# Feed-forward of a decoder trunk: one plain unit, four seven-product units in a row, the half unit last

## The reference

```
def swiglu(x, w_gu, w_down):          # x: 256 x 1024 after an RMS norm
    gate, up = jnp.split(x @ w_gu, 2, axis=-1)      # w_gu: 1024 x 5632
    return (jax.nn.silu(gate) * up) @ w_down        # w_down: 2816 x 1024
```

## Time and profile before

| | |
|---|---|
| device time, median of 3 runs | 2020.74 us (2019.19 to 2021.62) |
| the profiled execution's own time | 2019.88 us |
| its span in the profile | 2018.0 us |
| granted TensorE clock over the span | 1.0 of full (2.4 GHz) |
| PE busy | 1998.2 us, 10299 matmuls |
| DVE, ACT, POOL busy | 1566.5, 1187.3, 168.7 us |

### The profile page before, as it was taken

One profiled execution on the slowest core, in us unless ns is written; L12 is line 12 of the kernel. 1 busy time (PEld: TensorE's weight loads), 2 busy tenths in 40 slices (PEclk: granted clock), 3 DMA queues, 4 the chain that ended last, 5 costly groups with the idle time before them and its releaser, 6 DMA issues.

```text
span 2018.0 us, 25283 instructions
## 1 busy us (share of the span) xinstructions
PE 1998.2 (99%) x10299; PEld 1705.1 (84%) x10299; DVE 1566.5 (78%) x1489; ACT 1187.3 (59%) x1269; POOL 168.7 (8%) x165
## 2 busy tenths in 40 slices
PE   7999999999999999999999999999999999999998
PEld 6888998888888899988888888988888888998887
DVE  6778567778886889968878878778878778568777
ACT  6546576556655676646556555446556556576555
POOL 2000001000000014410001000000001001001000
PEclk9999999999999999999999999999999999999999
DMA  8867535867787484368876867658876867535864
GB/s 275 257 226 229 184 105 138 252 235 229 232 248 210 139 274 132 126 229 239 242 217 194 245 241 193 206 189 248 248 219 188 253 222 232 178 105 142 256 229 114
DMA packets 242183, 419.87 MB, mean 208 GB/s; under 512 B 10668, under 2 KB 92932, under 8 KB 241556
## 3 DMA queue, kind: packets, MB, share of 16 engines
q1 hardware_dynamic: 215732, 363.34, 53.0%
q0 software_dynamic: 26048, 54.61, 15.0%
q10 hardware_dynamic: 288, 0.31, 0.0%
HBM read 417.14 MB, written 1.08 MB: 207 GB/s over the span
## 4 chain that ended last, share of the span: by engine, by line
PE 87%; DVE 7%; ACT 3%; issue 1%; DMA 1%; ACTq 0%; SPq 0%; POOLq 0%; POOL 0%; DVEq 0%
PE bank L1594 51%; PE bank L1735 23%; PE bank L1600 7%; DVE w_lo L1113 3%; PE bank L1769 2%; DVE arena L1461 2%; ACT w_hi L734 2%; PE bank L1627 1%; PE bank L1909 1%; PE bank L1940 1%; DMA stage<-in_ssd_w_in 0%; PE bank L1922 0%; ACT arena L1009 0%; DMA arena<-seg_rows 0%; DMA arena<-in_ffn_norm 0%
## 5 line engine op out<-in xcount | busy, mean ns | idle before, releaser
L1113 DVE TENSOR_TENSOR w_lo<-stage,w_hi 128x2048 fp32r<-128x2048 f32 (+1 forms) x224 | 514.8, 2300 | 152.4 <-ACT w_hi L734 151.2
L1113 DVE TENSOR_TENSOR w_lo<-arena,w_hi 128x2048 fp32r<-128x2048 f32 (+1 forms) x196 | 444.3, 2268 | 162.4 <-ACT w_hi L734 161.7
L734 ACT ACTIVATE w_hi<-stage 128x2048 fp32r<-128x2048 f32 (+1 forms) x224 | 423.3, 1892 | 207.5 <-PE bank L1594 141.7
L734 ACT ACTIVATE w_hi<-arena 128x2048 fp32r<-128x2048 f32 (+1 forms) x196 | 371.7, 1897 | 236.8 <-PE bank L1594 157.0
L1594 PE MATMUL bank<-w_hi,mt_hi 128*128 128x512 f32 x928 | 367.3, 396 | 0.4 <-DVE mt_lo L1347 0.4
L1594 PE MATMUL bank<-w_lo,mt_hi 128*128 128x512 f32 x928 | 361.5, 390 | 0.0
L1594 PE MATMUL bank<-w_hi,mt_lo 128*128 128x512 f32 x928 | 361.0, 390 | 0.0
L1594 PE MATMUL bank<-w_hi,xt_hi 128*128 128x512 f32 x704 | 279.2, 398 | 3.0 <-DVE w_lo L1113 1.3
L1594 PE MATMUL bank<-w_lo,xt_hi 128*128 128x512 f32 x704 | 274.8, 391 | 0.0
L1594 PE MATMUL bank<-w_hi,xt_lo 128*128 128x512 f32 x704 | 251.9, 390 | 0.0
L1594 PEld LDWEIGHTS bank<-w_hi,mt_lo 128*128 128x128 f32 x928 | 174.1, 188 | 37.0
(11 more groups left out here) (219 smaller groups left out, 2810.8 us busy)
## 6 DMA issues: line engine op xcount, KB each, us to landing
arena<-in_ffn_w_gu SPq DMA_DIRECT2D x81, 1024.0 KB, 5.3
stage<-in_ffn_w_gu SPq DMA_DIRECT2D x79, 1024.0 KB, 5.3
stage<-in_ffn_w_down SPq DMA_DIRECT2D x96, 512.0 KB, 5.0
arena<-in_ffn_w_down SPq DMA_DIRECT2D x80, 512.0 KB, 4.9
arena<-in_ffn_w_gu POOLq DMA_DIRECT2D x29, 1024.0 KB, 9.6
stage<-in_ffn_w_gu POOLq DMA_DIRECT2D x19, 1024.0 KB, 9.8
stage<-in_ffn_w_gu SPq DMA_DIRECT2D x18, 512.0 KB, 8.7
stage<-in_sb_w_qkv SPq DMA_DIRECT2D x16, 512.0 KB, 4.6
```

The source lines that it names most:

```text
L734: act.activation(w_hi[q][:, 0:c], stage[s][:, 0:c], ACT.Copy).then_inc(hi_done, 1)
L1113: dve.tensor_tensor(w_lo[q][:, 0:c], stage[s][:, 0:c], w_hi[q][:, 0:c].bitcast(F32), ALU.subtract).then_inc(lo_done, 1)
```

## The change

`UNITS` becomes "PSSSSH": four S units one behind the other, and the half unit last. `DOWNS` becomes (0, 1, 2, 2, 2, 1). For an S unit behind an S unit (`adjacent`) the first of its two down blocks is put between B11 and A1, and VectorE's sum for A1 is formed one step later, in the step whose next block is B11. The order is then 0G0 0G1 0U0 0U1, 1B11 1A1 1B22 0D0 1A3 1B21 1A2 1A4, 2B11 0D1 2A1 2B22 1D0 2A3 2B21 2A2 2A4, 3B11 1D1 3A1 3B22 2D0 3A3 3B21 3A2 3A4, 4B11 2D1 4A1 4B22 3D0 4A3 4B21 4A2 4A4, 5H0 5H1 3D1 4D0 4D1 5D0: 45 steps. Unit 1's hidden tile is transposed behind 2A1, and so on; unit 4's behind 5H0 and unit 5's behind 3D1.

```
-UNITS = "PSHSPS"
-DOWNS = (0, 2, 1, 2, 2, 1)
+UNITS = "PSSSSH"
+DOWNS = (0, 1, 2, 2, 2, 1)
...
+def adjacent(u):
+
+    return u > 0 and UNITS[u - 1:u + 1] == "SS"
...
         now, waiting = waiting[:DOWNS[u]], waiting[DOWNS[u]:]
-        order += own[:lead]
+        if adjacent(u):
+            order += own[:1] + now[:1]
+            order += own[1:lead]
+            now = now[1:]
+        else:
+            order += own[:lead]
...
+                    if i + 1 < len(FFN_ORDER):
+                        u, name = FFN_ORDER[i + 1]
+                        if name == "B11" and adjacent(u):
+                            weight_sum(u, "A1")
                     if i + 2 < len(FFN_ORDER):
                         u, name = FFN_ORDER[i + 2]
-                        if name == "B11":
+                        if name == "B11" and not adjacent(u):
                             weight_sum(u, "A1")
```

## The result

| | before | after |
|---|---|---|
| median of the runs, us | 2020.01 (2019.19 to 2021.62, 4 runs) | 2033.11 (2031.18 to 2033.51, 4 runs) |
| profiled execution: own time / span, us | 2019.88 / 2018.0 | 2033.51 / 2031.8 |

After over before is **1.0062, interval 1.0045 to 1.0079**: slower by 13.1 us in the medians, by 13.8 in the two profiled spans. The forecast was slower by 5.7 (2026.4 us), with a range of 2018 to 2042. So the sign is right and the size is less than half. The profiled execution of the kernel after is the slowest of its four, so what is read from its trace is some 0.5 to 1.2 us more than the medians give.

A forecast was written before the change was run, and what follows sets the result against it. PE, busy 99%, was taken to set the time. From the profiled 2019.88: -21.8 + 26.6 + 0.8 = +5.7, so 2025.5; with the runs' median 0.86 higher, 2026.4 us, range 2018 to 2042.

The forecast's parts named there:

- The saving: On PE, 12 fewer product matmuls of 0.2267 us in each of 8 feed-forwards: 21.8 us less.
- The boundary: At A1 between S units, PE waits for the split behind the moved sum: 1.11 us, 24 times, 26.6 us.
- The 0.11 of restart: At A1 after PE's wait, second matmul 0.34 us behind the first instead of 0.23: 0.11 us more per boundary.
- The short waits: First matmul behind an A4 waits for PSUM release: two more places per feed-forward, 0.05 us each, 0.8 us.
- The queues that are moved past: SP's loads and POOL's accumulating DMAs in the new order: loads costed at nothing, median landings add nothing beyond 1.11 us.
- Z - 10.6: Cost per boundary of the A2 accumulate landing after Z: nothing at 10.5 us, 1.6 at 12.2.
- The formulas for both loops: Unit time through the accumulating DMAs: L + 22.4 us for A3's, Z + 20.25 for A2's, against PE's 30.86.
- rival 3: Accumulating DMAs land late among the plain loads, 2.6 us at two boundaries per feed-forward: 2050 us; chance 0.18 (2030 to 2055).
- its upper end: Longest landings at two of three boundaries, 1.6 us each: 34.5 us instead of 26.6, about 2034 us.
- Covered: Rival 1: DVE reaches A1 by 185.37, PE doesn't wait, kernel faster at 1999 us; chance 0.14, covered or partly so.
- Even: Rival 2: restart free and A1 wait 0.8 to 1.07 us, time 2018 to 2024.8; chance 0.24 (2016.7 to 2024.8).
- the spare 1.3 us of DVE per unit: DVE needs 29.6 us per S unit against PE's 30.86; the spare was claimed not to help at the boundary.

The follow-up runs named there:

- the two runs that take them away: Kernel after with three plain loads held until the second accumulate landed, 2026.47 us; kernel after with both accumulating DMAs cut to 64 columns, 2028.43 us.
- the halves: Kernel after with A1's sum, both splits and PE's product at S-unit boundaries in two halves of 1024 columns: 2036.78 us, ratio 1.008.
- the first four runs: Kernel after with: A1 boundary sum one column wide, 2063.05 us; accumulating DMAs of 64 columns, 2028.43; S units in pairs, 2035.89; sum and splits in halves, 2036.78.
- without the A1 sum: Kernel after with VectorE's boundary sum for A1 one column wide instead of 2048, waits and DMAs unchanged: 2063.05 us.
- the hold: Kernel after with SP holding back three plain loads until the second accumulating DMA has landed: 2026.47 us, ratio 1.003.

## Why the prediction was right, and where it was short

**The saving**, 21.8 us: right. The product matmuls are 96 fewer, and their pace between waits hasn't changed, 0.23 us start to start (74.67, then 74.91 and 75.14). The other price named, 131 ns, would have made 12.6; no run shows that pace. What the prediction says at the end of that paragraph, that down blocks and transposes change nothing, doesn't hold: the number of hidden tiles stays, but for 16 more of them a product block follows the transposes, at 0.15 us each, 2.4 us.

**The boundary**, 26.6 us: right in place, mechanism and the times of each event. 24 waits stand at A1 behind a down block, behind ACT's split and the weight sum. The runs price it at 23.8 us, or 25 by the units' own times. The 0.11 of restart is there (0.33 us to the second matmul). The wait is 1.00 against the plain count of blocks; against the last matmul ahead of it (73.20, next due at 73.43) it is 0.91, because 0.09 had already been lost on the way. I had counted that 0.09 into the chain, and it belongs to the next term.

**The short waits**, 0.8 us: right for the places that it names (two behind an A4 before, four now, 0.05 us each), too small as the sum of all small losses, which is 5.3 us. 2.4 of them are the steps behind the transposes. With the chain it is 29.1 against 27.4: a miss of 1.7 only because the chain was put too high and the small losses too low, which is luck.

**The queues that are moved past**, nothing: this step failed, with 7.0 us. It failed in two sentences. One took the landing Z of the second accumulate from the kernel before at its median, 10.5; it is 11.8 in the new order. The other costed SP's loads at nothing because each comes in good time. That was the wrong question: what counts is not that a load is late, but that it makes another DMA late. By my own formula, Z - 10.6, a landing of 11.8 costs 1.2 us, hardly above the 1.11 that PE waits anyway, and one of 13.0 costs 2.4. So the 7.0 us are an excess at some boundaries only, 0.44 us in the mean over the 16. The formulas for both loops were right, as the units' times show; what was wrong is the Z put into one. This is rival 3's mechanism at a smaller size than its 2050. I had set it against the forecast as the one or the other; both hold together. The nearest that the prediction came is its upper end with the longest landings, 2034.

The terms found: -21.8 + 23.8 + 5.3 + 7.0 = +14.3. They are differences of bodies one from the next, so they add up by their making, and they hold for this order of taking things away (the DMAs first, then the chain). Taken away first, the chain gives a loss of 29 us.

**Rivals.** Covered (1999) is where the kernel gets only when both limits are lifted, 2002. Even (2018 to 2024.8) isn't reached without the late DMAs either: the two runs that take them away give 2026.5 and 2028.4. For the spare 1.3 us of DVE per unit the prediction said that it lies on the other side of the chain; the halves show it, since with the DMAs out of the way they win 24.5 us with DVE's work unchanged.

**What I had wrong after the result.** That the chain's price could be had back by shortening or avoiding the chain alone. Three of the first four runs were built on that, and all three lost.

## What to carry to other kernels

When a wait on the critical path goes, what it covered comes up next: before shortening a chain, look up how much later each DMA that runs beside it may land. Ask of every plain load not only whether it is in time, but what is in flight when it starts; a load with time to spare can be held back, in the kernel before at no measured cost (2020.59 against 2020.31), and in the kernel with the halves that one wait turned a loss of 16.5 us into a gain of 11.8. Where a loop closes over a DMA, put the longest landings into its formula beside the median, and expect the landings to change with the order. A change that loses by itself can be the better one behind another fix, so an order is judged once the limit that it meets has been taken away.

## What the runs showed of the hardware

The first of two accumulating DMAs of 1 MB, with the second issued 4.3 us behind it, lands 8.4 to 8.8 us after its issue in the median of most kernels here (11.5 without the A1 sum, 10.8 there with the hold); a plain one lands in 5.2 to 5.7. In the kernel after, three plain loads, 1 MB and twice 0.5 MB, issued 2 to 5 us behind the second accumulate make that one 2.3 us later (11.8 against 9.5). With the same hold it lands 1.0 earlier in the kernel before (9.5 for 10.5) and 3.0 earlier in the one without the A1 sum (11.8 for 14.8).

A matmul behind a wait of PE for an operand is followed after 0.33 to 0.34 us instead of 0.23, and a matmul of a product block starts 0.18 us behind a transpose where one of a plain or down block starts 0.03 behind it.

While the accumulates run, the DMA engines are full at a low rate; by stretches in the kernel after (the last three columns are PE's clock, the DMA share and GB/s; the share passes 1 since a packet is counted whole in the stretch in which it starts):

```profile
74.60:79.00 4.40, 4.40 (x24) 3.60 (x24) 4.40 (x3) 3.04 (x5) 1.24 (x1) 1.00 1.12 202
...
86.40:90.00 3.60, 3.60 (x17) 3.00 (x16) 3.59 (x2) 2.55 (x2) 0.00 (x0) 1.00 1.03 408
```

In the first stretch both accumulates and a plain load are in flight, in the second plain loads alone: the same full engines, at twice the bytes.
